# Second attention of a two-block model: where the row scores and key scores lie in PSUM, and in which order TensorE takes them

## The chip, the core and the metric

One core of a Trainium2 chip runs the whole program. The metric is the device time of one execution in microseconds; lower is better. TensorE (PE in the profile) multiplies, VectorE (DVE), ScalarE (ACT) and the pool engine (POOL) do the rest, SyncE (SP) issues most transfers. The accumulators of TensorE, PSUM, are one tile `ps` of 8 banks, each 512 fp32 wide on 128 partitions.

## What is computed

Two layers of a hybrid block (attention beside a recurrent unit, MLP, a gated projection), then two layers of a second model: a state-space mixer, and an attention mixer with context. The change touches the attention of the latter alone:

```python
qc, kc, vc, gc = project(h_ctx)
ql, kl, vl, gl = project(h_lat)
k_all = jnp.concatenate([kc, kl], axis=1)
v_all = jnp.concatenate([vc, vl], axis=1)
s = jnp.einsum('bqgrd,bkgd->bgrqk', q, k) * (A_HEADDIM ** -0.5)
p = jax.nn.softmax(s, axis=-1)
o = jnp.einsum('bgrqk,bkgd->bqgrd', p, v)
```

There are 16 query heads on 4 key heads of 64 features, 512 queries (the latent rows) and 768 keys (256 of context, 512 latent). The results are gated, projected and added, and a norm ends the program.

## The kernel before, in words

Eight rounds b = 0..7 (`PAIRS`) take two query heads each, one on partitions 0 to 63 (e = 0) and one on 64 to 127 (e = 1). Every softmax needs the maximum of each query's scores, so scores are computed twice.

**Row scores** (`row_scores(r)`, line 1163; r = 4b + t for the queries 128t to 128t+127 of round b): queries on partitions, keys along the row, in one fp32r pass. Four matmuls of 64 contracted rows, for each head 512 and 256 keys, into banks 4 and 5 (e = 0) and 6 and 7 (e = 1). VectorE takes the negated maximum over the 768 keys of both heads (`maximum(r)`, line 2805), and only then may the next row scores start, since they use the same banks (`pe.wait_ge(mx_r, r)`). There are 32 of them. Seven are computed ahead inside the last two gate tiles, whose matmuls are those of line 1107 (`ahead_row`); the others stand at `ROW_SLOTS` of the rounds, until they run out in round 6.

**Turn** (`turn_max(b)`, line 1178): four small matmuls turn the maxima of a round's four rows into rows of PSUM, VectorE spreads them into the low part of q (`max_rows`, line 2816). It waits for the maxima 4b to 4b+3.

**Key scores** (`key_scores(b, kb)`, lines 1200 and 1205): keys on partitions, the 512 queries along the row, for each head a half block of two matmuls 128*128 (high part, then the corrections and the maximum). Half e goes to bank e, so half n = 2(6b + kb) + e waits for the exponential of half n - 2, which frees the bank. A key block is both halves of one kb; a round has six. ScalarE takes the exponential of each half into `pT2`, a ring of four blocks (`probs`, line 1955); the pool engine adds the blocks of a round up (line 473).

**Value sums** (`attend(b, i)`, line 1218): eight matmuls 128*64 over key blocks 2i and 2i+1, into bank 2 over the three i of a round; they wait for those exponentials. After the third, VectorE reads bank 2 (`gated(b)`, line 2824). **Probability sums** (`prob_sums(b)`, line 1232): four matmuls from the pool's sum, in the round after.

The order is written out by hand: TensorE's is the loop below (`slot` puts row scores where its name is in `ROW_SLOTS`), VectorE's this, with m(r) for `maximum(r)`: gated(b-1), m(4b+7), o_lo(b-3) (line 2833), in even rounds k_split (line 2794), m(4b+8), normed(b-2) (line 2829), max_rows(b+1), m(4b+9), m(4b+10). ScalarE has, beside the exponentials, key copies (lines 1918, 1920) in even rounds, query copies (1907), reciprocals of the probability sums (1961, 1963) after block 1, and `o_hi` (1967) after block 5. SP loads the next but one round's q by DMA, once the key scores that used the buffer are done. In round 0 the first exponential follows the tanh of the last gate tile and a load of the exponential's table.

Of the kernel before, what the change touches and what calls it, by code (L numbers as in the profile page):

```python
# [21 lines left out]
ACT = mybir.ActivationFunctionType  # L22
AX = mybir.AxisListType

P = 128
# [3 lines left out]
S = 512  # L29
# [22 lines left out]
T = CTX + S  # L52
# [13 lines left out]
UNITS = QH * 4  # L66
PAIRS = QH // 2
RING = 4
ROW_SLOTS = ("0E", "1V", "2K", "2E")

C2_GF, C2_NW, C2_MB, C2_FN, C2_CP, C2_MN, C2_DTB, C2_QN, C2_KN = 0, 8, 24, 72, 80, 272, 288, 289, 290
NP2 = 291
# [27 lines left out]
def build(nc, io):  # L100
# [8 lines left out]
    h = at("h", 48, [P, KB, S])  # L109
# [124 lines left out]
    pT2 = [at(f"pT2{i}", 80 + 4 * i, [P, 2, S]) for i in range(RING)]  # L234
    Q1 = [at(f"Q1{i}", 164 + 4 * i, [P, 2, S], F32R) for i in range(2)]
    QL = [at(f"QL{i}", 172 + 4 * i, [P, 2, S], F32R) for i in range(2)]
    qrow = at("qrow", 64, [P, KB, S], F32R)
    qrest = at("qrest", 48, [P, KB, S], F32R)
    K1 = [at(f"K1{i}", 180 + 3 * i, [P, T], F32R) for i in range(2)]
    K2 = [at(f"K2{i}", 186 + 3 * i, [P, T], F32R) for i in range(2)]  # L240
    psum2 = [at(f"psum2{i}", 192 + 4 * i, [P, 2, S]) for i in range(2)]
    nm = at("nm", 205, [P, PAIRS, 2, 4])
# [12 lines left out]
    ps = nc.alloc_psum_tensor("ps", [P, 8, 512], F32)  # L255
    TWO = lambda s: ps[:, 2 * s:2 * s + 2, :]

    def sem(name):
        return nc.alloc_semaphore(name)
# [37 lines left out]
    s_ps, mx_r, nm_ps, mr_r = sem("row_scores"), sem("max_ready"), sem("max_turned"), sem("max_rows")  # L297
    sT_ps, pT_r, pad_r = sem("key_scores"), sem("probs"), sem("probs_added")
# [6 lines left out]

    def MAX_BANK(b):
        return 3 if b else 1

    def LAND(b):
        return 16 + (16 * 6 * (b // 2) if b % 2 == 0 else 16 * 2 + 16 * 6 * (b // 2))  # L310
# [192 lines left out]
    def _(pe):  # L503
# [52 lines left out]
        for l in range(DEPTH):  # L556
# [164 lines left out]
            b = 0  # L721
# [44 lines left out]
        for b in range(KB):  # L766
# [3 lines left out]
            j = 32 * (b % 4)  # L770
            mm = pe.matmul(ps[j:j + 2, 5, :], gf2[:, b, :], hsqr[:, b, :], start=(b < 4), stop=(b >= 4))
# [3 lines left out]
        for c in range(4):  # L775
            mm = pe.matmul(ps[:, 4, 2 * c:2 * c + 2], srow[:, c * P:(c + 1) * P], misc[:, 4:6], start=True, stop=True)
# [3 lines left out]
        for n in range(2):  # L780
            for c in range(4):
                q = 16 + 4 * n + c
                mm = pe.matmul(ps[:, 6 + n, c * P:(c + 1) * P], dcol[:, q:q + 1].broadcast_to([P, P]), ident[:, :],
                               start=True, stop=True)
# [92 lines left out]
        for d, tri in enumerate((triF, triB)):  # L877
# [3 lines left out]
                  start=True, stop=True).then_inc(dt_p, 1)  # L881
# [267 lines left out]
        def row_scores(r):  # L1149

            b, t, j = r // 4, r % 4, r // 8
            if t == 0:
                pe.wait_ge(q_hi, b + 1)
                pe.wait_ge(k_hi, 2 * j + 2)
            if r:
                pe.wait_ge(mx_r, r)
            else:
                pe.wait_ge(rp_rd, 10)
            for n, (k0, k1) in enumerate(((0, S), (S, T))):
                for e in range(2):  # L1160
                    h = slice(64 * e, 64 * e + 64)
                    q = Q1[b][h, e, t * P:(t + 1) * P] if b < 2 else qrow[h, b, t * P:(t + 1) * P]
                    mm = pe.matmul(ps[:, 4 + 2 * e + n, 0:k1 - k0], q, (K1 if e else K2)[j % 2][h, k0:k1],  # L1163
                                   start=True, stop=True)
            mm.then_inc(s_ps, 1)

        def turn_max(b):

            pe.wait_ge(mx_r, 4 * b + 4)
            if b == 0:  # L1170
                pe.wait_ge(g_rd, 3)
            else:
                pe.wait_ge(mr_r, b)
                pe.wait_ge(g_rd, 4)
            if b >= 3:
                pe.wait_ge(rc_r, 2 * (b - 3) + 1)
            for e in range(2):
                mm = pe.matmul(ps[64:68, MAX_BANK(b), e * P:(e + 1) * P], nm[:, b, e, :], ident[:, :], start=True, stop=True)
            mm.then_inc(nm_ps, 1)

        def key_scores(b, kb):

            j, p = b // 2, b % 2
            ks = slice(kb * P, (kb + 1) * P)
            if kb == 0:
                pe.wait_ge(k_lo, j + 1)
                pe.wait_ge(clears, 3 if b else 2)
                if b >= 2:
                    pe.wait_ge(land[p], LAND(b))
                else:  # L1190
                    pe.wait_ge(q_hi, b + 1)
            for e in range(2):
                n = 2 * (NC * b + kb) + e
                if n >= 2:
                    pe.wait_ge(pT_r, n - 1)
                elif e == 0:
                    pe.wait_ge(g_rd, 3)
                else:
                    pe.wait_ge(mr_r, 1)
                pe.matmul(ps[:, e, :], K1[j % 2][:, ks], Q1[p][:, e, :], start=True, stop=False)  # L1200
                if kb == 0 and e == 0:
                    pe.wait_ge(mr_r, b + 1)
                    if b == 1:
                        pe.wait_ge(land[1], LAND(1))
                pe.matmul(ps[:, e, :], K2[j % 2][:, ks], QL[p][:, e, :], start=False, stop=True).then_inc(sT_ps, 1)  # L1205

        def attend(b, i):

            pe.wait_ge(pT_r, 2 * (NC * b + 2 * i + 2))
            if i == 0:  # L1210
                if b:
                    pe.wait_ge(o_ev, b)
                else:
                    pe.wait_ge(g_rd, 4)
            j = b // 2
            for kb in range(2 * i, 2 * i + 2):
                for e in range(2):
                    mm = pe.matmul(ps[64 * e:64 * e + 64, 2, :], vtok2[:, kb, HD * j:HD * j + HD],  # L1218
                                   pT2[(NC * b + kb) % RING][:, e, :], start=(kb == 0), stop=(kb == NC - 1))
            mm.then_inc(o_ps, 1)  # L1220

        def prob_sums(b):

            last = b + 1 == PAIRS
            pe.wait_ge(pad_r, 5 * b + (4 if last else 5))
            pe.wait_ge(mr_r, min(b + 3, PAIRS))
            if last:
                pe.wait_ge(rc_r, 2 * (b - 1) + 1)
            parts = [psum2[b % 2]] + ([pT2[(NC * b + NC - 1) % RING]] if last else [])
            for n, x in enumerate(parts):  # L1230
                for e in range(2):
                    mm = pe.matmul(ps[64 * e:64 * e + 64, 3, :], ones[:, 0:HD], x[:, e, :], start=(n == 0),
                                   stop=(n == len(parts) - 1))
            mm.then_inc(sum_ps, 1)
# [3 lines left out]
        def slot(b, where):  # L1238
            if where in ROW_SLOTS:
                r = next(rows, 4 * PAIRS)  # L1240
                if r < 4 * PAIRS:
                    row_scores(r)

        ahead_row = lambda: row_scores(next(rows))
        g_tile(2, {(0, 3): ahead_row, (0, 7): ahead_row, (1, 3): ahead_row, (1, 6): ahead_row})
        g_tile(3, {(0, 2): ahead_row, (0, 6): lambda: (turn_max(0), ahead_row()), (1, 3): ahead_row})
        for b in range(PAIRS):
            for i in range(3):
                key_scores(b, 2 * i)
                slot(b, f"{i}K")  # L1250
                if b or i:
                    attend(b - (i == 0), (i - 1) % 3)
                if i == 2 and b:
                    prob_sums(b - 1)
                slot(b, f"{i}V")
                key_scores(b, 2 * i + 1)
                slot(b, f"{i}E")
                if b + 1 < PAIRS and i == 1:
                    turn_max(b + 1)
        attend(PAIRS - 1, 2)  # L1260
        prob_sums(PAIRS - 1)

# [33 lines left out]
    def _(act):  # L1296
        L = Ls
        A = act.activation
# [15 lines left out]
        for l in range(DEPTH):  # L1314
# [232 lines left out]
            for c in range(CHUNKS):  # L1547
                for j in range(4):
                    n = 4 * c + j
# [396 lines left out]
        def probs(b, kb):  # L1946

            g = NC * b + kb
            if g >= RING:
                old, ob = (g - RING) % NC, (g - RING) // NC  # L1950
                act.wait_ge(o_ps, 3 * ob + old // 2 + 1)
                act.wait_ge(pad_r, 5 * ob + max(old, 1))
            for e in range(2):
                act.wait_ge(sT_ps, 2 * g + e + 1)
                A(pT2[g % RING][:, e, :], ps[:, e, :], ACT.Exp).then_inc(pT_r, 1)

        def recips(b):

# [41 lines left out]
    def _(dve):  # L2000
        L = Ls
        V = dve
# [55 lines left out]
        for l in range(DEPTH):  # L2058
# [246 lines left out]
            for c in range(CHUNKS):  # L2305
                for j in range(4):
                    n = 4 * c + j
# [493 lines left out]
                V.tensor_tensor(QL[0][0:64, e, :], qb_[r, 0, :], Q1[0][r, e, :].bitcast(F32), ALU.subtract)  # L2801

        def maximum(r):
            dve.wait_ge(s_ps, r + 1)
            V.tensor_reduce(nm[:, r // 4, :, r % 4], ps[:, 4:8, :].rearrange("p (e a) n -> p e (a n)", e=2)[:, :, 0:T],
                            AX.X, ALU.max, negate=True).then_inc(mx_r, 1)

        def max_rows(b):
# [45 lines left out]
        for r in range(4):  # L2854
            maximum(r)
        gate(2)
        maximum(4)
        max_rows(0)
        maximum(5)
        maximum(6)  # L2860
        gate(3)
# [294 lines left out]
```

## Time and profile before

| what | us |
|---|---|
| median of 3 executions | 2368.4 (2367.91 to 2371.32) |
| the profiled execution | 2368.97 |
| its span in the trace | 2367.2 |
| second attention: from the first key scores to the next projection | 2179.8 to 2308.4 |

The span runs from the first to the last instruction; what the execution's own time has over it lies around the program. Times in rows are counted from the span's start. In a timeline each row is one instruction or a few equal ones in a row: start, length, engine, line, operation, output and inputs, shapes; brackets give the engine's idle time before it and who ended it. A matmul's length includes its way through the array, so matmuls overlap: what one costs is the distance from its start to the next start. 128*128, 64*128 and 128*64 are the rows and columns of the array that it uses; of two matmuls with different shapes in a merged row one shape is shown. The granted clock is 1.00 of 2.4 GHz in the whole stage.

### The profile page before, as it was taken

What the parts mean: (1) busy time and instruction counts of PE and PEld (TensorE: products, weight loads), DVE (VectorE), ACT (ScalarE), POOL (GpSimd) and SP (SyncE); (2) the same over time, 40 slices, a digit from 0 to 9 for tenths busy, and PEclk for the clock granted to TensorE, in tenths of its full rate; (3) what the DMA queues carried; (4) which work ended last, traced back from release to release, by engine and by line L of the source; (5) the groups of instructions that cost most, each with busy time, mean ns of one, the idle gap of its engine ahead of it and who ended that gap; (6) DMA issues with size and microseconds to landing.
All of it is one profiled execution on the core that took longest, in us unless ns stands there. A gap on an engine that the chain in (4) does not pass through costs nothing.

```text
span 2367.2 us, 32220 instructions
## 1 busy us (share of the span) xinstructions
PE 2296.3 (97%) x11638; PEld 1897.5 (80%) x11638; DVE 1486.4 (63%) x1848; ACT 762.1 (32%) x1600; POOL 1430.7 (60%) x1260
## 2 busy tenths in 40 slices
PE   8999999999999999999999999999999998999998
PEld 6867888888777788888878899999999986776447
DVE  7965433444775543343477789789788787546653
ACT  3363210112333420110246333333333334532551
POOL 8727776768776487776876434344343351365885
PEclk9999999999999999999999999999999999999999
DMA  4322434443223133443332111110111112022212
GB/s 174 113 69 76 146 134 152 150 138 111 89 76 130 37 135 132 160 142 132 118 115 107 37 54 36 53 53 35 53 53 35 53 53 83 31 77 76 54 27 71
DMA packets 41888, 211.38 MB, mean 89 GB/s; under 512 B 5440, under 2 KB 9536, under 8 KB 22080
## 3 DMA queue, kind: packets, MB, share of 16 engines
q1 hardware_dynamic: 28032, 166.94, 20.2%
q10 hardware_dynamic: 13760, 43.07, 5.5%
q8 instruction: 71, 1.16, 0.2%
q14 instruction: 25, 0.20, 0.0%
HBM read 197.67 MB, written 7.34 MB: 87 GB/s over the span
## 4 chain that ended last, share of the span: by engine, by line
PE 77%; DVE 15%; issue 3%; ACT 2%; DMA 1%; POOL 1%; ACTq 0%; DVEq 0%; SPq 0%; POOLq 0%
PE ps L539 40%; PE ps L838 16%; PE ps L1107 5%; DVE convd L2434 2%; PE ps L1218 2%; PE ps L941 1%; PE ps L1200 1%; POOL wlo L428 1%; PE ps L635 1%; DVE wdec L2587 1%; PE ps L964 1%; PE ps L1205 1%; DVE convd L2430 1%; PE ps L1074 1%; PE ps L1163 1%
## 5 line engine op out<-in xcount | busy, mean ns | idle before, releaser
L424 POOL TENSOR_SCALAR whi<-wraw 128x512 fp32r<-128x512 f32 x564 | 384.5, 711 | 872.1 <-PE ps L838 363.4
L428 POOL TENSOR_TENSOR wlo<-wraw,whi 128x512 fp32r<-128x512 f32 x568 | 855.9, 1539 | 0.8 <-ACT whi L1457 0.8
L539 PE MATMUL ps<-uhi,whi 128*128 128x512 f32 x896 | 353.0, 394 | 12.4 <-DVE ulo L2091 8.0
L539 PE MATMUL ps<-uhi,wlo 128*128 128x512 f32 x896 | 349.3, 390 | 0.0
L539 PE MATMUL ps<-ulo,whi 128*128 128x512 f32 x896 | 349.2, 390 | 0.0
L838 PE MATMUL ps<-inhi,whi 128*128 128x384 f32 (+1 forms) x784 | 245.2, 346 | 7.2 <-DVE inlo L2399 3.2
L838 PE MATMUL ps<-inlo,whi 128*128 128x384 f32 (+1 forms) x784 | 237.4, 336 | 0.0
L838 PE MATMUL ps<-inhi,wlo 128*128 128x384 f32 (+1 forms) x784 | 237.2, 335 | 0.0
L539 PEld LDWEIGHTS ps<-uhi,whi 128*128 128x128 f32 x896 | 168.6, 188 | 51.0 <-POOL wlo L401 7.9
L539 PE MATMUL ps<-hidhi,whi 128*128 128x512 f32 x512 | 199.2, 389 | 0.0
L539 PE MATMUL ps<-hidhi,wlo 128*128 128x512 f32 x512 | 199.2, 389 | 0.0
L539 PE MATMUL ps<-hidlo,whi 128*128 128x512 f32 x512 | 199.2, 389 | 0.0
L2280 DVE TENSOR_TENSOR h<-h,ps 128x1024 f32<-128x1024 f32 x40 | 48.9, 1221 | 237.9 <-PE ps L539 237.9
L539 PEld LDWEIGHTS ps<-uhi,wlo 128*128 128x128 f32 x896 | 168.6, 188 | 36.1 <-issue 1.4
L539 PEld LDWEIGHTS ps<-ulo,whi 128*128 128x128 f32 x896 | 168.6, 188 | 35.3
L1553 ACT ACTIVATE hsq<-hm 128x1024 f32<-128x1024 f32 x32 | 34.0, 1062 | 488.3 <-DVE hm L2311 488.3
L838 PEld LDWEIGHTS ps<-inhi,whi 128*128 128x128 f32 (+1 forms) x784 | 144.1, 187 | 19.0 <-issue 8.7
L2434 DVE SCALAR_TENSOR_TENSOR convd<-raw,cpg,convd 128x770 f32<-128x770 f32 x128 | 147.8, 1154 | 3.2 <-ACT convd L1660 1.0
L2311 DVE SCALAR_TENSOR_TENSOR hm<-ps,rstd 128x1024 f32<-128x1024 f32 x32 | 39.2, 1225 | 173.3 <-PE ps L539 173.2
L838 PEld LDWEIGHTS ps<-inhi,wlo 128*128 128x128 f32 (+1 forms) x784 | 144.8, 188 | 1.0
L838 PEld LDWEIGHTS ps<-inlo,whi 128*128 128x128 f32 (+1 forms) x784 | 144.8, 187 | 0.6
L1771 ACT ACTIVATE ebuf<-ps,tabg 128x128 f32<-128x128 f32 x384 | 104.7, 388 | 116.1 <-PE ps L953 89.8
(453 smaller groups left out, 4617.6 us busy)
## 6 DMA issues: line engine op xcount, KB each, us to landing
wraw<-in_wstream SPq DMA_DIRECT2D x149, 1024.0 KB, 4.8
modraw<-in_modw ACTq DMA_DIRECT2D x48, 512.0 KB, 3.4
hspill<-hres ACTq DMA_DIRECT2D x1, 3072.0 KB, 9.7
hback<-hspill ACTq DMA_DIRECT2D x1, 3072.0 KB, 10.0
Q<-qrow SPq DMA_DIRECT2D x24, 128.0 KB, 2.3
crow<-in_crow ACTq DMA_DIRECT2D x2, 1024.0 KB, 4.9
QL<-qrest SPq DMA_DIRECT2D x14, 128.0 KB, 2.3
h<-in_x SPq DMA_DIRECT2D x2, 512.0 KB, 5.7
```

Source lines behind the costliest of these rows:

```text
L424: pool.tensor_scalar(whi[:, s, c], wraw[:, s, c], 1.0, 0.0, ALU.mult, ALU.add).then_inc(wraw_read, 1)
L428: ins = pool.tensor_tensor(wlo[:, s, c], wraw[:, s, c], whi[:, s, c].bitcast(F32), ALU.subtract)
L539: mm = pe.matmul(ps[:, 2 * bank + m, :], a[:, w, c:c + P], b[:, kb, :], start=(n == 0 and i == 0), stop=(n == KB - 1 and i == 2))
L635: pe.matmul(ps[:, SCORE_BANKS(n)[c], 0:w], q, proj[64 * c:64 * c + 64, K0 + hd, 0:w], start=True, stop=False)
L838: mm = pe.matmul(ps[0:width, q + half, 0:HALF], a[:, s, c:c + width], b[:, kb, half * HALF:(half + 1) * HALF], start=(n == 0), stop=(n == ...
L1107: mm = pe.matmul(ps[:, q + m, :], a[:, k % 2, c:c + P], b[:, kb, t0:t0 + S], start=(kb == 0 and i == 0), stop=(kb == KB - 1 and i == 2))
L1218: mm = pe.matmul(ps[64 * e:64 * e + 64, 2, :], vtok2[:, kb, HD * j:HD * j + HD], pT2[(NC * b + kb) % RING][:, e, :], start=(kb == 0), stop ...
L1553: A(hsq[n % 2][:, :, :], hm[n % 2][:, :, :], ACT.Square).then_inc(L["sqh_r"], 1)
L1771: ins = A(ebuf[:, d, r, :], ps[:, 4 + d, r * P:(r + 1) * P], ACT.Exp, bias=tabg[:, K_NB + 2 * c + d, r:r + 1])
L2280: V.tensor_tensor(h[:, 2 * j:2 * j + 2, :], h[:, 2 * j:2 * j + 2, :], TWO(bank), ALU.add).then_inc(L["h_r"], 1)
L2311: V.scalar_tensor_tensor(out=hm[n % 2][:, :, :], in0=TWO(n % 2), scalar=0.0, in1=rstd2, op0=ALU.max, op1=ALU.mult).then_inc(L["m_r"], 1)
L2434: ins = V.scalar_tensor_tensor(out=o, in0=r[:, n:n + CW], scalar=cpg[:, 6 * b + n:6 * b + n + 1], in1=o, op0=ALU.mult, op1=ALU.add)
```

## The change

Row scores lie packed in banks 4 to 6: head 0 in bank 4 and the left half of bank 5, head 1 in the right half of bank 5 and in bank 6. The four matmuls come in another order (256 keys of head 0, 512 of head 1, 512 of head 0, 256 of head 1), and the last one waits for the first, as both write bank 5; the semaphore `s_ps` now counts three per row. Bank 7 is free by this and becomes the third bank of the key scores: half n goes to bank 0, 1 or 7 and waits for the exponential of half n - 3. The order of TensorE's blocks changes. With K for a key block, R for row scores, V for a value sum, T for the turn, P for probability sums, a round was

```
before: K0 V K1 R | K2 V R K3 T | K4 R V P K5 R
after:  K0 R V K1 | K2 R V T K3 | K4 R V P R K5
```

so that K1 and K2, K3 and K4, K5 and the next K0 stand side by side. VectorE's and ScalarE's orders stay as they are.

```diff
--- before.py
+++ after.py
@@ -66,7 +66,7 @@
 UNITS = QH * 4
 PAIRS = QH // 2
 RING = 4
-ROW_SLOTS = ("0E", "1V", "2K", "2E")
+ROW_SLOTS = ("0K", "1K", "2K", "2V")
 
 C2_GF, C2_NW, C2_MB, C2_FN, C2_CP, C2_MN, C2_DTB, C2_QN, C2_KN = 0, 8, 24, 72, 80, 272, 288, 289, 290
 NP2 = 291
@@ -306,6 +306,9 @@
     def MAX_BANK(b):
         return 3 if b else 1
 
+    def KEY_BANK(n):
+        return (0, 1, 7)[n % 3]
+
     def LAND(b):
         return 16 + (16 * 6 * (b // 2) if b % 2 == 0 else 16 * 2 + 16 * 6 * (b // 2))
 
@@ -1156,13 +1159,15 @@
                 pe.wait_ge(mx_r, r)
             else:
                 pe.wait_ge(rp_rd, 10)
-            for n, (k0, k1) in enumerate(((0, S), (S, T))):
-                for e in range(2):
-                    h = slice(64 * e, 64 * e + 64)
-                    q = Q1[b][h, e, t * P:(t + 1) * P] if b < 2 else qrow[h, b, t * P:(t + 1) * P]
-                    mm = pe.matmul(ps[:, 4 + 2 * e + n, 0:k1 - k0], q, (K1 if e else K2)[j % 2][h, k0:k1],
-                                   start=True, stop=True)
-            mm.then_inc(s_ps, 1)
+            for e, k0, k1, o in ((0, S, T, S), (1, 0, S, 1024), (0, 0, S, 0), (1, S, T, 768)):
+                h = slice(64 * e, 64 * e + 64)
+                q = Q1[b][h, e, t * P:(t + 1) * P] if b < 2 else qrow[h, b, t * P:(t + 1) * P]
+                if o == 768:
+                    pe.wait_ge(s_ps, 3 * r + 1)
+                mm = pe.matmul(ps[:, 4 + o // 512, o % 512:o % 512 + k1 - k0], q, (K1 if e else K2)[j % 2][h, k0:k1],
+                               start=True, stop=True)
+                if o != 1024:
+                    mm.then_inc(s_ps, 1)
 
         def turn_max(b):
 
@@ -1191,18 +1196,18 @@
                     pe.wait_ge(q_hi, b + 1)
             for e in range(2):
                 n = 2 * (NC * b + kb) + e
-                if n >= 2:
-                    pe.wait_ge(pT_r, n - 1)
-                elif e == 0:
+                if n >= 3:
+                    pe.wait_ge(pT_r, n - 2)
+                elif n == 0:
                     pe.wait_ge(g_rd, 3)
-                else:
+                elif n == 1:
                     pe.wait_ge(mr_r, 1)
-                pe.matmul(ps[:, e, :], K1[j % 2][:, ks], Q1[p][:, e, :], start=True, stop=False)
+                pe.matmul(ps[:, KEY_BANK(n), :], K1[j % 2][:, ks], Q1[p][:, e, :], start=True, stop=False)
                 if kb == 0 and e == 0:
                     pe.wait_ge(mr_r, b + 1)
                     if b == 1:
                         pe.wait_ge(land[1], LAND(1))
-                pe.matmul(ps[:, e, :], K2[j % 2][:, ks], QL[p][:, e, :], start=False, stop=True).then_inc(sT_ps, 1)
+                pe.matmul(ps[:, KEY_BANK(n), :], K2[j % 2][:, ks], QL[p][:, e, :], start=False, stop=True).then_inc(sT_ps, 1)
 
         def attend(b, i):
 
@@ -1253,10 +1258,9 @@
                 if i == 2 and b:
                     prob_sums(b - 1)
                 slot(b, f"{i}V")
-                key_scores(b, 2 * i + 1)
-                slot(b, f"{i}E")
                 if b + 1 < PAIRS and i == 1:
                     turn_max(b + 1)
+                key_scores(b, 2 * i + 1)
         attend(PAIRS - 1, 2)
         prob_sums(PAIRS - 1)
 
@@ -1952,7 +1956,7 @@
                 act.wait_ge(pad_r, 5 * ob + max(old, 1))
             for e in range(2):
                 act.wait_ge(sT_ps, 2 * g + e + 1)
-                A(pT2[g % RING][:, e, :], ps[:, e, :], ACT.Exp).then_inc(pT_r, 1)
+                A(pT2[g % RING][:, e, :], ps[:, KEY_BANK(2 * g + e), :], ACT.Exp).then_inc(pT_r, 1)
 
         def recips(b):
 
@@ -2801,8 +2805,8 @@
                 V.tensor_tensor(QL[0][0:64, e, :], qb_[r, 0, :], Q1[0][r, e, :].bitcast(F32), ALU.subtract)
 
         def maximum(r):
-            dve.wait_ge(s_ps, r + 1)
-            V.tensor_reduce(nm[:, r // 4, :, r % 4], ps[:, 4:8, :].rearrange("p (e a) n -> p e (a n)", e=2)[:, :, 0:T],
+            dve.wait_ge(s_ps, 3 * r + 3)
+            V.tensor_reduce(nm[:, r // 4, :, r % 4], ps[:, 4:7, :].rearrange("p a n -> p (a n)").rearrange("p (e n) -> p e n", e=2),
                             AX.X, ALU.max, negate=True).then_inc(mx_r, 1)
 
         def max_rows(b):
```

## Rows read from the trace of the kernel before

**Rows 1.** The page of the whole execution, its busy line.

```profile
PE 2296.3 (97%) x11638; PEld 1897.5 (80%) x11638; DVE 1486.4 (63%) x1848; ACT 762.1 (32%) x1600; POOL 1430.7 (60%) x1260
```

**Rows 2.** Windows: one line for each stretch, busy us (instructions) of PE, PEld, DVE, ACT, POOL; clock; DMA.

```profile
2179.80:2196.50 16.70, 14.47 (x67) 6.90 (x65) 10.76 (x7) 11.84 (x19) 13.35 (x7) 1.00 0.09 21
2196.50:2276.30 79.80, 79.77 (x361) 36.01 (x360) 55.08 (x40) 44.20 (x81) 68.44 (x32) 1.00 0.22 50
2276.30:2308.40 32.10, 30.31 (x126) 12.31 (x125) 14.55 (x13) 17.55 (x33) 27.43 (x15) 1.00 0.10 23
```

**Rows 3.** Timeline of TensorE in round 4: start us, length us, line, operation, count.

```profile
2246.14 0.50 PE L1200 MATMUL ps<-Q,K 128*128 128x512 f32 x1
...
2249.08 1.94 PE L1218 MATMUL ps<-pT,vtok 128*64 128x512 f32 x8
2250.95 0.61 PE L1163 MATMUL ps<-K,qrow 64*128 64x512 f32 x4
2251.49 0.50 PE L1200 MATMUL ps<-Q,K 128*128 128x512 f32 x1
2251.83 0.40 PE L1205 MATMUL ps<-QL,K 128*128 128x512 f32 x1
2252.06 0.39 PE L1200 MATMUL ps<-Q,K 128*128 128x512 f32 x1
...
2252.62 0.60 PE L1178 MATMUL ps<-ident,nm 128*4 128x128 f32 x4
2253.15 0.50 PE L1200 MATMUL ps<-Q,K 128*128 128x512 f32 x1
...
2254.81 1.94 PE L1218 MATMUL ps<-pT,vtok 128*64 128x512 f32 x8
...
2257.56 0.50 PE L1200 MATMUL ps<-Q,K 128*128 128x512 f32 x1
```

**Rows 4.** Timeline of all engines in round 7, around a wait for an exponential.

```profile
2293.25 0.40 PE L1205 MATMUL ps<-QL,K 128*128 128x512 f32 x1
...
2293.76 1.09 ACT L1955 ACTIVATE pT<-ps 128x512 f32<-128x512 f32 x2 [1.90 <-PE ps L1205]
...
2294.41 0.50 PE L1200 MATMUL ps<-Q,K 128*128 128x512 f32 x1 [0.30 <-ACT pT L1955]
2294.52 0.19 PEld L1205 LDWEIGHTS ps<-QL,K 128*128 128x128 f32 x1
```

**Rows 5.** Source view of line 1163: durations in ns, least, median, most.

```profile
L1163 PE MATMUL ps<-K,qrow x96: 275/384/501, 2187.9 to 2279.7; 64*128 64x512 f32 x48, 64*128 64x256 f32 x48
```

**Rows 6.** Timeline of VectorE in round 4.

```profile
2246.26 0.69 DVE L2824 SCALAR_TENSOR_TENSOR qb<-ps,gs 128x512 f32<-128x512 f32 x1 [1.25 <-PE ps L1218]
...
2249.61 1.76 DVE L2833 TENSOR_TENSOR olo<-qb,ohi 128x512 fp32r<-128x512 f32 x1
2251.40 0.95 DVE L2794 TENSOR_TENSOR K<-kf,K 64x768 fp32r<-64x768 f32 x1
...
2254.05 1.10 DVE L2829 TENSOR_TENSOR qb<-qb,gs 128x512 f32<-128x512 f32 x1
2255.18 1.22 DVE L2816 TENSOR_TENSOR QL<-ps,ident 4x1024 fp32r<-4x1024 f32 x1
2256.43 1.76 DVE L2805 TENSOR_REDUCE nm<-ps 128x2 f32<-128x1536 f32 x1
```

**Rows 7.** Groups by line in rounds 1 to 5: count, busy us, mean ns.

```profile
L473 POOL TENSOR_TENSOR psum<-psum,pT 128x1024 f32<-128x1024 f32 x22 | 54.6, 2480 | 3.7 <-ACT pT L1955 1.8
```

**Rows 8.** Timeline of TensorE at the stage's start.

```profile
2182.98 0.50 PE L1200 MATMUL ps<-Q,K 128*128 128x512 f32 x1 [2.12 <-ACT pT L1955]
```

**Rows 9.** Timeline of TensorE at the stage's end.

```profile
2289.96 0.47 PE L1200 MATMUL ps<-Q,K 128*128 128x512 f32 x1 [0.40 <-ACT pT L1955]
...
2291.04 1.94 PE L1218 MATMUL ps<-pT,vtok 128*64 128x512 f32 x8
...
2304.79 1.51 PE L1218 MATMUL ps<-pT,vtok 128*64 128x512 f32 x6 [0.79 <-ACT pT L1955]
```

## The prediction

> **What bounds the kernel now.** I read the page's busy line first [rows 1]: TensorE is busy 97% of the span, every other engine 63% or less. The change touches only the second attention's eight rounds, so I cut that stage out by windows [rows 2]. In the 79.80 us between the third value sum of round 0 and that of round 5, TensorE is busy 79.77 us: 15.96 us a round with no hole, while ScalarE works 44.20 and VectorE 55.08 us. So in the middle rounds whatever TensorE is spared comes off the time and whatever it is given goes on; the exponentials, which the third bank is to free, hold nobody there. Holes stand at the start (16.70 us with 14.47 busy) and in the last stretch (32.10 with 30.31). Third, the timeline of one round [rows 3], for the cost of each block as the distance from its start to the next block's start. A value sum takes 1.87 us, row scores 0.54, a turn 0.53, the value sum with the probability sums behind it 2.75. A key block takes 1.13: its second matmul starts 0.34 after the first, the third 0.23 after that, but the fourth and the change to the next block take 0.56 (2252.06 to 2252.62), where two plain steps would be 0.47. So each entry into and exit from a stretch of 128*128 matmuls costs about 0.1 us.
>
> **Part 1, two key blocks in a row.** Two blocks apart cost 2 x 1.13 = 2.26 us, side by side 1.13 + 4 x 0.235 = 2.07. But the fourth half waits for the exponential of the first. That half ends 0.34 + 0.40 = 0.74 after the block's start; where ScalarE idles the exponential starts 0.11 after such an end (2293.65 to 2293.76), lasts 0.60 (two in 1.09), and TensorE starts 0.05 after its end (2294.36 to 2294.41) [rows 4]: its weight load can go at 1.50, its matmul 0.1 later, against 1.51 unhindered. So I take 2.15 us a pair: three pairs a round save 3 x (2.26 - 2.15) = 0.32 us. Bounds: 0 saved if ScalarE is late, 0.57 if the fourth half is not held. ScalarE is not late by my count: it is idle for 35 of the 80 us, and what is queued on it before a pair ends over 0.5 us before the pair's first half.
>
> **Part 2, the wait inside row scores.** The four matmuls are now 256 and 512 columns side by side on the two row halves, then 512 and 256, and the last one, with its weight load, waits for the end of the first, since both write bank 5. Both halves still stream 768 columns, so a gain is excluded. Before: the block's last pair ends 0.61 after its start and lasts 0.275 [rows 3, 5], so it starts at 0.34 and the next block 0.20 later. After: a 256-column matmul that opens a block lasts 0.275 plus the 0.11 by which an opening 512-column one is longer (0.50 against 0.39 [rows 3]): it ends at 0.385. With the 0.05 us of [rows 4] the last weight load goes at 0.435, now with nothing in front of it to hide it: a load starts the stream of its matmul 0.11 later (2294.41 to 2294.52, when the next load may follow [rows 4]). Then 0.20 as before: the block takes 0.75, 0.20 more. Ends: 0 if the release comes before 0.34, 0.31 if it comes only with the 512-column partner's end at 0.50 (0.50 + 0.05 + 0.11 + 0.20 = 0.86 against 0.54). I take 0.20, since each piece has a row. Of the 32 blocks one (row 7) lies in a wait, 24 are in the sums of part 3, and the seven that run ahead inside the gate tiles pay it in full: 7 x 0.20 = +1.4 us. VectorE hears of a block's end at 0.435 + 0.385 = 0.82 instead of 0.61, which I follow below.
>
> **Part 3, the order.** Row scores 4b+7 now stand before the third value sum of round b-1, but VectorE's program is unchanged: it first reads that value sum (L2824), then takes the maximum of row 4b+7. And row 4b+8 may not start before this maximum, since all rows share their banks. Call a the end of the value sum. The read starts at a + 0.12 (2246.14 to 2246.26, [rows 3, 6]) and lasts 0.69, the maximum follows at 0.03 and lasts 1.76, TensorE hears 0.05 later: a + 2.65. TensorE arrives at a + 2.15, with the pair of key blocks behind it. It stands still 0.50 us in each of the rounds 1 to 5, and turn, value sum and the other pairs are queued behind. Before the change a key block and then the row lay after the value sum, with VectorE free at a + 0.81 and the row at a + 1.13: no hold. Further down the list nothing is late. The old value's correction 1.76, the key correction 0.95, a maximum 1.76, the gating 1.10, the negated maxima 1.22 and the next maximum 1.76 [rows 6] end at a + 11.2; row 4b+10 comes at a + 2.65 + 0.75 + 1.87 + 0.53 + 2.15 + 0.75 + 2.75 = a + 11.45. That is 0.2 us of room in round 4, and over 1 in the odd ones. From row 4b+10 to 4b+11 TensorE has 0.75 + 2.15 = 2.90, VectorE needs 0.82 + 0.04 + 1.76 + 0.05 = 2.67. The pool engine, 68.44 us of 79.80 busy [rows 2] with adds of 2.48 us [rows 7], fits a longer round. No DMA is moved; SP's loads of the next q wait for the last key block two rounds before their use and keep a round of room.
>
> **The sum.** One middle round after: 1.87 + 2.65 + 0.75 + 1.87 + 0.53 + 2.15 + 0.75 + 2.75 + 0.75 + 2.15 + 0.75 = 16.97, less 0.03 for the value sum with its sums, which averages 2.72: 16.94, or 15.96 + 0.80 + 0.50 - 0.32. I take 16.9, so five rounds give **+4.7 us**. Round 0: before, TensorE waits 2.1 us for the first exponential, until 2182.98 [rows 8]; that exponential follows the gate tile's tanh and does not move by itself. Now row 7 and a first half of key block 1 go into this wait, for the new bank needs no release; but the second half waits for the same exponential, and block 2's last half for one more, behind a key copy, until 2184.84. Walking on with the lengths above, row 8 starts at 2185.5, the value sums at 2186.25, 2191.55 and 2197.1, the last against 2196.5 in [rows 2]: **+0.65**, of which 0.8 are the four waits of part 2. Round 6 has no rows left after the first: before, 2276.3 to 2291.04, 14.7 us [rows 2, 9]; after, 1.87 + 2.15 + 1.87 + 0.53 + 2.15 + 2.72 + 2.15 = 13.45: **-1.3**. Here and in round 7 the old kernel already has key blocks side by side, and with two banks the third half waits for an exponential (0.40 at 2289.96 [rows 9], two more like it in round 7). Round 7: 13.75 before (2291.04 to 2304.79), 1.87 + 2.15 + 1.87 + 2.15 + 2.72 + 1.98 (the last half's exponential: 0.81 + 0.40 + 0.11 + 0.60 + 0.05) = 12.74 after: **-1.0**. The pool's four last adds would end 3.9 + 4 x 2.5 = 13.9 us into that stretch; the sum that needs them starts at 14.5. With the rows ahead, +1.4: 1.4 + 0.65 + 4.7 - 1.3 - 1.0 = **+4.5 us**. The profiled execution has a span of 2367.2 and took 2368.97 us, 0.6 above the median of 2368.4; the sum on the median is **2372.9 us**. A measurement here can tell about 0.2% from no change, 4.7 us: the forecast lies just inside that, so half of its own spread is beyond.
>
> **The rivals.**
> *The release comes with the partner's end.* What decides is the wait of part 2. If the first matmul's end is not seen until its 512-column partner is through, each row block costs 0.31 more and not 0.20: 31 blocks x 0.11 = +3.4 more, **2376.3 us**, slower. The mechanism passes the 0.2% bound from 0.21 us a block on. No pair of unequal length is in the trace of before. The Trainium skill ("TensorE: Matmul & The Clock Gate", Part 3, what overlaps and what doesn't) has matmuls start and end strictly in program order, with no difference of ends in its traces; read strictly that ties nothing earlier than the partner, read loosely it is this rival, and no run here shows it yet.
> *The wait costs nothing*, because the release is there by 0.34: 31 x 0.20 = 6.2 less, **2366.7 us**, no change to be measured. Against it: 0.385 and 0.05 each have a row.
> *Faster.* As the last one, and VectorE's hold is not there either (2.5 us) and the fourth halves run unheld (15 x 0.08 + 0.5): 2366.7 - 4.2 = **2362.5 us**. It needs three of my readings to be wrong, one of them the program order of VectorE.
> *VectorE's list slips.* Beside the pool's its operations vary (two of one shape took 1.76 and 1.10 [rows 6]), and room in round 4 is 0.2 us. A slip of 0.4 us a round gives +2, **2374.9 us**, slower.
>
> **How the numbers follow.** Forecast 0.55, of which 0.25 fall beyond +0.2% and 0.30 within; partner's end 0.17, slower; wait free 0.15, no change; slip 0.07, of which 0.05 slower; faster 0.06. That makes slower 0.47, same 0.47, faster 0.06. The range runs from just above the free wait, 2367.0, to just above the partner's end, 2377.5.
>
> **What would show it.** Row scores at 0.75 from start to next start, their last load 0.43 after the first; pairs of key blocks at 2.15; VectorE named as releaser of row scores some 0.5 us five times; rounds of 16.9 us in the middle, 13.4 and 12.7 at the end; maxima still 1.76. Middle rounds at 16 or less would sink the forecast, and so would row scores at 0.55, or a hold before a value sum or a turn that I have not named.

## Result, and the profile after

| | before | after |
|---|---|---|
| median | 2368.6 us (5 executions) | 2380.4 us (5) |
| ratio | | 1.0053, 95% interval 1.0042 to 1.0065 |
| span of the profiled execution | 2367.2 | 2378.6 |

The change costs 11.8 us, 0.5%. The forecast was +4.5 and the range ended at 2377.5, so the size is wrong by 7.3 us and the time lies outside. First the stage by windows of the changed kernel, cut at the same blocks as [rows 2] (busy us and instructions of PE, PEld, DVE, ACT, POOL, then TensorE's clock): first key scores to the third value sum of round 0, the five middle rounds, the rest of the stage.

```profile
2181.10:2203.60 22.50, 18.80 (x71) 8.97 (x69) 11.79 (x7) 12.40 (x20) 14.15 (x8) 0.85 0.08 18
2203.60:2289.20 85.60, 82.92 (x363) 39.75 (x362) 59.40 (x39) 42.49 (x80) 67.15 (x31) 1.00 0.20 46
2289.20:2319.80 30.60, 29.35 (x122) 12.18 (x121) 14.96 (x12) 16.93 (x33) 25.96 (x13) 1.00 0.10 23
```

The first stretch took 16.7 us before and takes 22.5, with a mean clock of 0.85. The middle took 79.8 with 79.77 busy; it takes 85.6 with 82.92 busy: not only is there more work, TensorE also stands still for 2.7 us. The rest, counted to the end of the last sums, took 32.05 and takes 30.6. The seven rows ahead of the stage take 0.75 us each instead of 0.54: from the first of them to the first key scores it is 26.99 us and was 25.50, 1.5 more. The stretches and these rows make 5.8 + 5.8 - 1.5 + 1.5 = 11.6 us; the spans differ by 11.4.

TensorE in round 1, to be held against [rows 3] (now L1205 and L1210 are the key scores, L1167 row scores, L1223 value sums, L1183 the turn):

```profile
2205.45 0.50 PE L1205 MATMUL ps<-Q,K 128*128 128x512 f32 x1
2205.79 0.40 PE L1210 MATMUL ps<-QL,K 128*128 128x512 f32 x1
...
2206.95 0.50 PE L1205 MATMUL ps<-Q,K 128*128 128x512 f32 x1
2207.29 0.40 PE L1210 MATMUL ps<-QL,K 128*128 128x512 f32 x1
2208.07 0.79 PE L1167 MATMUL ps<-K,qrow 64*128 64x256 f32 x4 [0.38 <-DVE nm L2809]
2208.79 1.94 PE L1223 MATMUL ps<-pT,vtok 128*64 128x512 f32 x8
2210.66 0.60 PE L1183 MATMUL ps<-ident,nm 128*4 128x128 f32 x4
2211.19 0.50 PE L1205 MATMUL ps<-Q,K 128*128 128x512 f32 x1
...
2213.35 0.82 PE L1167 MATMUL ps<-K,qrow 64*128 64x256 f32 x4
2214.10 1.94 PE L1223 MATMUL ps<-pT,vtok 128*64 128x512 f32 x8
```

Two key blocks side by side take 2.16 us (2211.19 to 2213.35), the row scores behind them 0.75 (2213.35 to 2214.10; 0.54 before), a value sum 1.87 as ever. After the first pair, which ends 2.16 behind 2205.45, TensorE stands until 2208.07, and the view names VectorE's maximum (L2809). All of this was forecast, the block lengths to 0.01 us. The wait inside row scores shows in the weight loads of such a block. The last line is from the view of line 1167, for the row scores ahead of the stage and row 7: least, median and longest duration of their matmuls in ns:

```profile
2236.96 0.62 PEld L1167 LDWEIGHTS ps<-K,qrow 64*128 64x128 f32 x4 [0.37 <-DVE nm L2809]
2236.96 0.82 PE L1167 MATMUL ps<-K,qrow 64*128 64x256 f32 x4
...
L1167 PE MATMUL ps<-K,Q x32: 379/385/498, 2154.1 to 2182.6; 64*128 64x256 f32 x16, 64*128 64x512 f32 x16
```

The four loads end 0.62 after the first start (0.30 in the kernel before) and one lasts 0.18, so the last goes at 0.44, as forecast (0.435). The 256-column matmul that opens the block lasts 0.38 us and has ended by then, its 512-column partner lasts 0.49 (0.50 in the blocks ahead) and has not: the load is released by the first one's end.

What was not forecast stands in round 0:

```profile
2182.11 0.82 PE L1167 MATMUL ps<-K,Q 64*128 64x256 f32 x4
2182.86 0.50 PE L1205 MATMUL ps<-Q,K 128*128 128x512 f32 x1
...
2184.30 0.50 PE L1205 MATMUL ps<-Q,K 128*128 128x512 f32 x1 [0.71 <-ACT pT L1959]
...
2186.14 0.50 PE L1205 MATMUL ps<-Q,K 128*128 128x512 f32 x1 [0.61 <-ACT pT L1959]
2186.47 0.40 PE L1210 MATMUL ps<-QL,K 128*128 128x512 f32 x1
2189.25 1.21 PE L1167 MATMUL ps<-K,qrow 64*128 64x256 f32 x4 [2.38 <-ACT qrow L1911]
2190.39 3.68 PE L1223 MATMUL ps<-pT,vtok 128*64 128x512 f32 x8
2194.00 1.02 PE L1183 MATMUL ps<-ident,nm 128*4 128x128 f32 x4
2194.95 0.70 PE L1205 MATMUL ps<-Q,K 128*128 128x512 f32 x1
2195.48 0.40 PE L1210 MATMUL ps<-QL,K 128*128 128x512 f32 x1
```

Row scores 8 (2189.25) come 2.4 us after key block 2 is done, and the releaser is L1911, ScalarE's copy of q for round 2 (`row_q(2)`). Row 8 is the first of round 2's rows, and `row_scores` waits for that copy (`q_hi`). ScalarE makes it in round 0 behind the exponentials of key block 2; the new order has put the row before the value sum, where the copy is not there yet. The trace of before shows the same copy and the row behind it:

```profile
2187.25 0.63 ACT L1907 ACTIVATE qrow<-qb 128x512 fp32r<-128x512 f32 x1
...
2187.93 0.30 PEld L1163 LDWEIGHTS ps<-K,qrow 64*128 64x128 f32 x4 [0.92 <-ACT qrow L1907]
```

The copy ended at 2187.88 and the row's weight loads went 0.05 later: even in its old place the row was held by it, for some 0.1 us of TensorE's time (the value sum ahead of it took 1.98 us to the next start and not 1.87). The prediction put the row at 2185.5 on this same scale, 2.4 us before the copy's end, and that is the stand.

Then the value sum takes 3.61 us and the turn 0.95, nearly twice their length, with nothing named that they wait for. The windows say why:

```profile
2181.10:2189.20 8.10, 4.45 (x17) 2.23 (x15) 4.62 (x3) 7.76 (x11) 4.89 (x3) 0.96 0.14 32
2189.20:2197.00 7.80, 7.75 (x24) 3.46 (x24) 3.65 (x3) 1.09 (x3) 2.88 (x1) 0.60 0.00 0
```

The mean clock of the second stretch is 0.60: after standing for 3.65 of the 8.1 us before, TensorE ran for most of it at the lower level, 1.2 GHz. In the profile of before no such fall lies in this stage [rows 2], although TensorE stood 2.1 us there too [rows 8].

### The profile page after: what moved, and what is told of

Read it like the earlier page. It is cut to its first block, busy times and chain, and to the rows that moved or that the text cites. A ratio compares the mean times of both kernels' runs of the same rounds, so it can differ in the third digit from the quotient of the medians.

```text
span 2378.6 us, 32220 instructions
## 1 busy us (share of the span) xinstructions
PE 2303.7 (97%) x11638; PEld 1904.1 (80%) x11638; DVE 1493.0 (63%) x1848; ACT 760.4 (32%) x1600; POOL 1429.3 (60%) x1260
## 4 chain that ended last, share of the span: by engine, by line
PE 75%; DVE 16%; issue 3%; ACT 3%; POOL 2%; DMA 1%; ACTq 0%; DVEq 0%; SPq 0%; POOLq 0%
PE ps L542 39%; PE ps L841 16%; PE ps L1110 5%; DVE convd L2438 2%; PE ps L1223 1%; PE ps L944 1%; PE ps L1167 1%; POOL wlo L431 1%; PE ps L638 1%; DVE wdec L2591 1%; PE ps L967 1%; POOL psum L476 1%; DVE convd L2434 1%; PE ps L1077 1%; DVE offs L2608 1%
```

## The experiments

Times of whole executions scatter by some 0.1%, and a stage's length is read to 0.01 us, so I compare stretches of the profiled executions, in the same three parts; the medians stand beside them. The stage runs from the first key scores to the end of the last probability sums.

| kernel | round 0 | rounds 1 to 5 | rest | stage | ratio to before (95%) |
|---|---|---|---|---|---|
| before | 16.7 | 79.85 | 32.05 | 128.6 | |
| changed | 22.5 | 85.6 | 30.6 | 138.7 | 1.0053 (1.0042 to 1.0065) |
| e1_row8_late | 17.85 | 85.6 | 30.6 | 134.0 | 1.0031 (1.0020 to 1.0041) |
| e2_fill_stand | 21.75 | 85.6 | 30.5 | 137.9 | 1.0038 (1.0024 to 1.0051) |
| e5_fill_right | 19.7 | 85.6 | 30.5 | 135.8 | 1.0031 (1.0020 to 1.0043) |
| e3_max_first | 21.2 | 84.2 | 29.9 | 135.2 | 1.0036 (1.0022 to 1.0050) |
| e11_copies_early | 22.5 | 88.1 | 30.6 | 141.2 | one execution |
| e4_pack_only | 18.7 | 83.8 | 32.3 | 134.8 | 1.0035 (1.0023 to 1.0048) |
| e6_order_only | 21.5 | 86.7 | 32.3 | 140.6 | 1.0047 (1.0033 to 1.0060) |
| e7_all_mended | 17.05 | 82.5 | 29.85 | 129.4 | 1.0006 (0.9997 to 1.0016) |
| e8_old_order_tail | 17.8 | 79.8 | 30.6 | 128.2 | 0.9989 (0.9980 to 0.9998) |
| e9_tail_banks | 16.7 | 79.85 | 30.6 | 127.1 | 0.9996 (0.9987 to 1.0005) |
| e10_tail_row7 | 19.5 | 79.85 | 30.6 | 129.9 | 0.9991 (0.9982 to 1.0000) |

Kernels with packed rows have 1.5 us more ahead of the stage. What else lies ahead of it shifts by up to 5 us between the profiled executions, which is why ratios and stages do not match to 0.1%. Each stage is read from one execution, and where the clock fell in it, it need not have fallen in the others.

**Is it row 8?** Edit to the changed kernel:

```diff
-            if where in ROW_SLOTS:
+            if where in (ROW_SLOTS if b else ("0K", "1V", "2K", "2V")):
```

> The changed kernel, but in round 0 row scores 8 stand behind the first value sum, not before it; all else as changed. Theory A (the unforeseen 5 us lie in round 0: row 8 needs the copy of q that ScalarE makes after key block 2's exponentials, TensorE stands 2.4 us for it, and the granted clock, which reads 0.83 over the stretch of that stand, then costs some 2.6 us more): the third value sum of round 0 comes about 5 us earlier, clock 1.00 there, 2375.5 us in all. Rival B (round 0 only shows first what the new order costs anyway; taken away there, the wait comes back at the next row): less than 1.5 us gained, 2379 or more.

Round 0 takes 17.85 us and not 22.5, the clock is 1.00 in it, and rounds 1 to 5 stay to 0.02 us. The stage is 4.7 us shorter (5 expected; row 8 still stands 0.5 us for the copy), the median 2376.3. The wait did not come back elsewhere.

**Stand and clock apart.** Matmuls into a bank that is free then, ahead of row 8, with the stand itself left:

```diff
...
+            if r == 8:
+                pe.wait_ge(g_rd, 4)
+                busy(FILL, 3)
             if t == 0:
                 pe.wait_ge(q_hi, b + 1)
```

> The changed kernel with 20 small matmuls into a bank that nobody uses at that time, ahead of row scores 8 in round 0, so that TensorE works through its 2.4 us stand and the stand itself stays. Theory A (half of the loss in round 0 is the clock that falls after the stand): clock 1.00 through the stage, 2.6 us gained, 2377.8 us. Rival B (the clock's fall has another cause, or its cost lies beside other waits): clock still 0.83 in that stretch, or under 1 us gained.

With FILL = 20 this missed its aim: the 20 were issued as 40 matmuls and took 4.56 us, so that row 8 began 2 us later than in the changed kernel. The clock was 1.00 all the same; the length says nothing. Again with 10:

> The changed kernel with 10 small matmuls ahead of row scores 8 in round 0 (the 20 of the run before were issued as 40 and took 4.5 us, longer than the stand). Theory A (the granted clock falls because TensorE stands): 2.3 us of filling, row scores 8 start no later than in the changed kernel, clock 1.00 in the stage, the first value sum takes 1.87 and not 3.6 us: 2.6 us gained over the changed kernel. Rival B: the clock falls all the same, nothing gained.

Its timeline, and its windows in the place of the ones above:

```profile
2186.09 2.40 PE L517 MATMUL ps<-ident 128*128 128x128 f32 x20
2188.63 0.82 PE L1171 MATMUL ps<-K,qrow 64*128 64x256 f32 x4
2189.38 1.94 PE L1227 MATMUL ps<-pT,vtok 128*64 128x512 f32 x8
2191.24 0.60 PE L1187 MATMUL ps<-ident,nm 128*4 128x128 f32 x4
```

```profile
2180.50:2188.60 8.10, 6.67 (x37) 4.63 (x35) 4.64 (x3) 7.75 (x11) 4.91 (x4) 1.00 0.14 32
2188.60:2197.00 8.40, 8.37 (x40) 3.87 (x40) 5.40 (x4) 2.58 (x5) 6.17 (x3) 1.00 0.01 2
```

Row 8 begins 8.13 us after the first key scores (8.14 in the changed kernel), and now the value sum takes 1.87 and the turn 0.53. Round 0 is 2.8 us shorter, 2.6 expected. So the 5.8 us that round 0 lost are 2.8 of clock, 2.4 of stand and 0.6 for all the rest of the change there, and that rest is what the prediction had (+0.65). Shown is that the fall goes when TensorE is kept at work through the stand. The mean clock of whole executions, those without a profile among them, says the same: 0.994 or 0.995 in all five of the changed kernel, 0.996 or 0.997 in the five of e2_fill_stand and the seven of e5_fill_right. The size of the fall is not fixed: in e3_max_first, with the same stand, the first value sum took 2.96 us and not 3.61, and round 0 21.2 us and not 22.5.

**The middle: whose stands?** VectorE's list turned round in the changed kernel:

```diff
-            if b:
-                gated(b - 1)
             if b + 1 < PAIRS:
                 maximum(4 * b + 7)
+            if b:
+                gated(b - 1)
```

> The changed kernel, but VectorE takes the maximum of row 4b+7 before it reads the value sum of round b-1. Theory A (in the odd rounds TensorE stands 0.45 us before row 4b+8 for this maximum; in rounds 2 and 4 a key copy of ScalarE holds the same row as long or longer): rounds 1, 3 and 5 are 0.45 us shorter each, rounds 2 and 4 keep 0.7 and 1.0 us of stand, now named for ScalarE's key copy; 1.35 us in all, 2379.1 us. Rival B (VectorE's hold is the whole of it in all five rounds): 2.9 us gained, 2377.5.

The pair of key blocks with the stand behind it took, in rounds 1 to 5, 2.62, 2.91, 2.62, 3.18 and 2.62 us in the changed kernel; here 2.16, 2.91, 2.17, 3.17 and 2.17. So VectorE's maximum holds the odd rounds for 0.45 us (forecast 0.50) and is not what ends the stand in rounds 2 and 4. The last value sum of round 6 with the sums behind it fell from 3.41 to 2.73 too, since the negated maxima, for which the sums wait, were ready. Then the key copies, also in the changed kernel:

```diff
-                if kb < 2 and more_k:
-                    split_k(b // 2 + 1, kb)
+                if kb < 2 and b == 0:
+                    split_k(1, kb)
+                if kb == 0 and b and more_k:
+                    split_k(b // 2 + 1, 0)
+                    split_k(b // 2 + 1, 1)
```

> The changed kernel, but in rounds 2 and 4 ScalarE makes both key copies behind the exponentials of key block 0, not one behind block 0 and one behind block 1. Theory A (row scores 16 and 24, the first on a new key head, stand for the second copy): the pair of key blocks and the stand behind it, 2.91 us in round 2 and 3.18 in round 4, fall to the 2.62 of the odd rounds, which VectorE's maximum sets; nothing else moves in them by over 0.2 us. Rival B (these stands are VectorE's, lengthened by the pool engine beside it): they stay at 2.9 and 3.2.

Both fell to 2.62. That is theory A for the stand. But "nothing else moves" was wrong: round 4, though its first stand was 0.56 us shorter, took 20.4 us and not 17.6, and has lost 3.3 at another place. VectorE's timeline there, and two windows of the same stretch:

```profile
2256.56 1.75 DVE L2812 TENSOR_REDUCE nm<-ps 128x2 f32<-128x1536 f32 x1
2258.22 2.53 DVE L2840 TENSOR_TENSOR olo<-qb,ohi 128x512 fp32r<-128x512 f32 x1
2260.79 3.02 DVE L2801 TENSOR_TENSOR K<-kf,K 64x768 fp32r<-64x768 f32 x1
2263.73 1.75 DVE L2812 TENSOR_REDUCE nm<-ps 128x2 f32<-128x1536 f32 x1
```

```profile
2261.50:2266.30 4.80, 3.07 (x16) 1.84 (x14) 4.77 (x3) 2.58 (x5) 4.21 (x3) 1.00 0.00 0
2266.30:2271.50 5.20, 5.20 (x18) 1.61 (x17) 3.25 (x3) 0.00 (x0) 3.70 (x2) 0.67 0.00 0
```

The corrections L2840 and L2801, beside the pool engine's adds, took 2.53 and 3.02 us, where [rows 6] have 1.76 and 0.95 for them and the changed kernel had 2.81 and 0.95 in this round; the maximum behind them (2263.73) came late, the next row scores stood 1.73 us for it, and the clock fell behind that stand (mean 0.67 in the second window). This is the slip that the prediction had as a rival, in one round of one execution: with VectorE's list this full, what it is read beside decides.

**Packing alone**, in the kernel before (new row scores with their wait, two key banks, old order):

```diff
...
+                if o == 768:
+                    pe.wait_ge(s_ps, 3 * r + 1)
...
```

> The kernel before with the packed row scores alone (three banks, the new order of four matmuls, the wait of the last for the first), key scores in two banks and the old order of blocks. Theory A (the wait costs 0.20 us in each of 31 blocks, on the path): row scores 0.75 us start to start, 6.2 us slower than before, 2374.8. Rival B (the wait is hidden wherever TensorE would have waited anyway; the loss comes from the order): under 3 us slower.

Rounds 1 to 5 take 83.80 us, all of them busy:

```profile
2198.50:2282.30 83.80, 83.80 (x361) 39.79 (x360) 53.84 (x40) 44.22 (x81) 68.23 (x31) 1.00 0.21 48
```

That is 3.95 more than before for 20 row blocks, 0.20 each. Round 0 has four of them, 0.8 us, and lost 2.0: in this execution the clock fell behind the old wait for the first exponential (mean 0.71 over the next 5.9 us), though that wait is 2.12 us as before. The median is 8.0 us above before, 6.2 expected.

**The order alone**, in the kernel before (rows in four banks, key scores in two):

```diff
-ROW_SLOTS = ("0E", "1V", "2K", "2E")
+ROW_SLOTS = ("0K", "1K", "2K", "2V")
...
-                key_scores(b, 2 * i + 1)
-                slot(b, f"{i}E")
                 if b + 1 < PAIRS and i == 1:
                     turn_max(b + 1)
+                key_scores(b, 2 * i + 1)
```

> The kernel before with the new order of blocks alone: row scores in four banks with one count, key scores in two banks. Theory A: row scores 0.55 us; a pair of key blocks 2.65 us, since with two banks its third half waits for an exponential, where three banks give 2.17; so a middle round takes about 17.2 us with 0.3 to 0.5 more in rounds 2 and 4, and round 0 has its stand: 10 to 12 us slower than before. Then the third bank is worth 0.5 us a pair, 9 us, and packing costs 6.3 for it. Rival B (the order itself is harmless and packing is all of the loss): under 4 us slower.

```profile
2210.67 0.50 PE L1200 MATMUL ps<-Q,K 128*128 128x512 f32 x1
...
2211.47 0.40 PE L1205 MATMUL ps<-QL,K 128*128 128x512 f32 x1
2212.17 0.50 PE L1200 MATMUL ps<-Q,K 128*128 128x512 f32 x1 [0.30 <-ACT pT L1954]
...
2213.32 0.62 PE L1163 MATMUL ps<-K,qrow 64*128 64x512 f32 x4
2213.87 0.65 PE L1218 MATMUL ps<-pT,vtok 128*64 128x512 f32 x2
```

A pair takes 2.65 us (2210.67 to 2213.32), with a stand for an exponential before its third half, and row scores 0.55. A middle round is 17.3 us against 15.97 before. So each half of the change fails without the other: in the new order the third bank is worth 0.49 us a pair (2.65 to 2.16), and it is paid with 0.20 in each row block. Three pairs win 1.47 us a round on e6_order_only and lose 0.8 for the four rows; against the old order, whose two blocks stood apart at 1.13 each, they win only 3 x 0.09. Round 0 of this kernel has the stand before row 8 too (1.90 us), and a slow value sum behind it (3.23 us).

**All stands mended**, in the changed kernel: VectorE's order as in e3_max_first, the key copies of rounds 2 and 4 as in e11_copies_early, those of round 0 before the last tanh, `row_q(2)` behind the first exponentials.

> The changed kernel with every stand that the order made taken away: VectorE takes maximum 4b+7 first, ScalarE makes the two key copies of an even round behind its first block's exponentials, those of round 0 before the last tanh, and the copy of q for row 8 behind the first exponentials. Row scores keep their inner wait. Theory A: middle rounds 16.4 us, all alike, no stand before row 8, clock 1.00 through the stage; the stage takes 130 us (128.6 before, 138.7 changed), and 1.4 come on top for the rows ahead: about 3 us slower than before. Rival B (a new wait takes their place): middle rounds above 16.7.

```profile
2201.10:2283.60 82.50, 82.50 (x361) 39.82 (x360) 59.26 (x39) 42.27 (x81) 66.31 (x31) 1.00 0.21 48
2283.60:2313.50 29.90, 29.11 (x122) 12.26 (x121) 12.61 (x12) 16.93 (x33) 25.71 (x13) 1.00 0.10 23
```

82.5 us for the middle, all busy, 16.5 a round; 129.4 for the stage, with 1.5 ahead of it: 2.3 us behind before; the ratio of 1.0006 has an interval across 1. In the middle nothing is left but the wait inside the row blocks: 79.85 + 20 x 0.20 - 15 x 0.09 = 82.5. This is the change with every stand of the middle taken away, and it does not beat the kernel before.

**What is free to take.** The last three kernels start from the one before. All three have the third bank where no packing is needed for it, from key block 4 of round 6 on, when bank 4 has no rows any more:

```diff
+    THREE = 2 * (NC * (PAIRS - 2) + 4)
+    def KEY_BANK(n):
+        return n % 2 if n < THREE else (0, 1, 4)[(n - THREE) % 3]
...
```

> The kernel before with what is free to take: in round 0 row scores 7 go into the wait for the first exponential, ScalarE copies earlier as in the run before, and from key block 4 of round 6 on, when no row scores are left, key scores turn among three banks (0, 1 and 4). Rows stay in four banks, the order of rounds 1 to 5 stays. Theory A: middle rounds 15.96 us, the three late pairs 2.17 instead of 2.6 us: about 2 us faster than before, 2366.7. Rival B (the end is bound by the pool's last adds, or the start by the exponential): under 0.8 us.

> The kernel before with the third bank alone, and only where it is free and where somebody waits: key scores turn among banks 0, 1 and 4 from key block 4 of round 6 on; nothing else is touched. Theory A: three late pairs of key blocks take 2.17 us instead of 2.60 to 2.69, the stage 127.1 us instead of 128.6, 1.5 us faster than before: 2367.2. Rival B (the time comes back before the last sums): under 0.5 us.

> As e9_tail_banks, and row scores 7 stand before key block 1 in round 0, in the wait for the first exponential. Theory A: 0.5 us more, the stage 126.6 us. Rival B (what made e8_old_order_tail give so little at the start was this, and not ScalarE's earlier copies): the first value sum starts no earlier after the first key block than 6.15 us, as before, or later.

```profile
2287.02 0.50 PE L1207 MATMUL ps<-Q,K 128*128 128x512 f32 x1
...
2288.05 0.40 PE L1207 MATMUL ps<-Q,K 128*128 128x512 f32 x1
...
2289.19 1.94 PE L1225 MATMUL ps<-pT,vtok 128*64 128x512 f32 x8
2291.06 0.51 PE L1207 MATMUL ps<-Q,K 128*128 128x512 f32 x1
```

The third halves start without a stand, a pair takes 2.17 us (2287.02 to 2289.19), and the rest of the stage 30.6 instead of 32.05 in all three. In e9_tail_banks nothing else moved: 127.1 us, 1.4 less than before. The stage shows it; the times of whole executions do not resolve it (ratio 0.9996, interval across 1). Row 7 in the wait of round 0 was a miss: in e10_tail_row7 the first value sum starts 7.03 us after the first key scores and not 6.15 as before. The row no longer takes its 0.68 us behind key block 1, but key blocks 1 and 2, now neighbours in two banks, stand once more, for 0.61 us, which gives the gain back, and the clock fell behind the two stands (mean 0.52 over the next 7 us): key block 2 took 2.0 us instead of 1.13 and the value sum 3.61. In e8_old_order_tail, with ScalarE's copies earlier, the second stand was 0.42 us, the value sum started at 6.82, and the clock fell as well (0.67 over 5 us). So the place of the row won nothing, and what round 0 lost here is the clock of one execution: that of e10_tail_row7 had a mean clock of 0.995, its ten others 0.996 or 0.997, so these may have lost less. The ratio of e8_old_order_tail below 1 is not explained by its stage, only 0.4 us shorter; that its median of 2366.8 met the 2366.7 expected is no proof of that sum. So e9_tail_banks is the version I would keep, for some 1.4 us.

## Why the prediction was wrong

Step by step, in the order in which it was put:

- *What bounds the kernel, block costs, part 1.* Right: pairs at 2.16 us against 2.15.
- *Part 2, the wait inside row scores.* Right, in place and size: 0.75 us a block, the last load at 0.44; measured are 1.5 us in the seven blocks ahead and 3.95 in the twenty of the middle (e4_pack_only). The rival of the partner's end is refuted by the load, that of a free wait by e4_pack_only.
- *Part 3, VectorE's hold.* Right for the odd rounds, 0.45 against 0.50. "It stands still 0.50 us in each of the rounds 1 to 5" was wrong for rounds 2 and 4, where ScalarE's second key copy ends the stand, at 0.75 and 1.0. "Further down the list nothing is late" failed by the same: the sums in round 4 came 0.16 late and those of round 6 0.68. Together the middle was forecast at +4.7 and came at +5.8, the rest at -2.3 and came at -1.5, 0.7 of the difference in the sums of round 6.
- *The sum, round 0: +0.65.* **This is the step that failed**, by 5.1 us out of 7.3. It walked row 8 into its new place with "row 8 starts at 2185.5" and asked only whether the bank was free. The row has two more conditions in its first lines, the copies of q and k for its head, and both are ScalarE's work of that same round. The trace of before had the dates: the copy of q ended at 2187.88, and the row followed it at 2187.93. Missing it hid 2.4 us of stand, and with it the fall of the clock, which cost 2.8 us more and for which the sum had no term at all, though it had TensorE standing earlier in the same round. The rest of round 0's term was right, +0.6 measured.
- *The rivals.* None was it. The range took in every price that had a row and none for a condition overlooked. That the time lies beyond it is not bad luck in the sizes but one wait of one instruction not looked up. The slip of VectorE's list came only in e11_copies_early, in one round.

That the time left over in the middle is the row blocks' wait and nothing else is shown by e7_all_mended; where e11_copies_early's slip comes from (the pool engine beside VectorE) is read from one execution and was not tested by itself. Open stays why stands of like length are followed by a fall of the clock in one execution and not in another.

## What to carry to other kernels

When a step is moved earlier, list every semaphore it waits for, also those that hardly held it in its old place, and date each in the new order; the trace of the old order has the dates. Here one wait of 0.1 us became one of 2.4. A stand of TensorE can have a second price behind it, the clock, so a forecast that leaves it idle for some 2 us needs a term for that and a chance: behind the 2.38 us stand of round 0 it fell in all three profiles that have it, and behind the 2.12 us wait of the old order in one of three. And a buffer bought with an inner wait in a block that runs 31 times on a full engine has to win more than that wait each time: here the third bank only paid where banks were free anyway.

## What the runs showed of the hardware that I had not expected

- After the same stand of 2.4 us the clock's fall cost different amounts (first value sum 3.61 us in the changed kernel, 2.96 in e3_max_first, 3.61 in e11_copies_early). After the 2.12 us wait at the stage's start it fell in e4_pack_only and not in the kernel before or in e9_tail_banks, and after stands of 1.58 and 0.61 us, or of 1.58 and 0.42, it fell in e10_tail_row7 and e8_old_order_tail. The Trainium skill ("TensorE: Matmul & The Clock Gate", Part 1) says that the moment of such a change varies from run to run, since the chip judges activity on a timing of its own that no kernel start resets; the trace agrees so far as equal stands cost different amounts, and shows nothing more of it.
- Two matmuls of unequal length side by side on the two row halves do not wait for each other's end: the 256-column one releases the weight load that waits for it at 0.44 us, while its 512-column partner runs to 0.49.
- A matmul of 128*128 on plain fp32 operands counts as two in the trace, 0.11 us each (20 for 10 issued in e5_fill_right), where each of the key scores' matmuls, on operands marked fp32r, counts as one.
